# A hybrid decoder step on one core: dt behind the short convolution, state transposes between state updates, placeholder rows in quarters

## The chip, the cores and the metric

The kernel runs on one core of a Trainium2 chip. A core has a matrix engine (TensorE, PE in the profile), VectorE (DVE), ScalarE (ACT), GpSimd (POOL) and a queue engine that issues most of the transfers (SyncE, SP); each follows its own instruction list and waits on semaphores. The metric is the device time of one execution in microseconds (us).

## The reference, cut to what matters

One layer for 528 prompt tokens (16 learned ones ahead of 512) and 64 sample tokens (8 sequences of 8), 592 in all, width 1024, all in float32:

```python
h = RMSNorm(x)
z, xbc, dt_raw, sc_b, sc_c, sc_h, g_ssd, g_sc = split(h @ w_in)   # dt_raw: 32 columns
xbc = silu(causal_conv4(xbc) + conv_b)
dt = softplus(dt_raw + dt_bias);  a_neg = -exp(A_log)
acum = cumsum(dt * a_neg)                # in chunks of 128 tokens
y, state = chunked_scan(x, dt, acum, B, C, state0) ; y += x * D
y_ssd = group_rmsnorm(y * silu(z)) @ w_ssd_out
y_sc = (sc_b * causal_conv3(sc_c * sc_h)) @ w_sc_out
x = x + (sigmoid(g_ssd) * y_ssd + sigmoid(g_sc) * y_sc) @ w_o
x = x + moe(RMSNorm(x))                  # 4 groups of 8 experts, top 1 group, top 2 experts
```

Final states and the last rows before each convolution are outputs too.

## The kernel before, in words

Each engine's program is written out by hand. The work is in stages.

**Start.** SyncE loads the first tile of rows, then eleven small vectors and the dt weights `wdt`, then the other four tiles, then the first weight blocks. Five tiles of 128 rows (the last has 80: 16 of the prompt and 64 of the samples) are normed: ScalarE sums the squares of a row and takes the root (`root`, L1425 and L1426), VectorE scales the rows (L1013), TensorE transposes them (L602), VectorE multiplies by the norm's weights into `hT` (L1004). A float32 product is then made of three faster ones: weights and activations are split into a rounded part (`w_hi`, `hT_hi`, by ScalarE, L1438 and L1444) and the rest (`w_lo`, `hT_lo`, a subtraction on GpSimd, L1691 and L1697). In the start all five row sums come first, then the first two weight roundings, then the five of h; GpSimd does the two weight subtractions and then the five of h. The dt product alone is made in plain float32, token tile by token tile (L610), then the small vectors are transposed (L617, L621), and VectorE and ScalarE make dt and dt*a of it.

**Blocks.** `pe_block` (L578) multiplies one block of 128 weight columns with all 592 tokens: 8 row tiles x 3 products x 2 halves of the tokens, 48 matmuls. Raw weights have two places in `ring`, and so do the split ones. When TensorE has finished block n, ScalarE rounds block n+2, GpSimd subtracts, and SyncE loads block n+4 into the place that came free. 24 blocks are the short convolution's (a loop of 4 turns of 6), 16 are the gate and `w_sc_out` (8 turns of 2), and the cumulative sums of dt stand between the two (L636 to L640).

**Groups.** Four turns of a loop follow, one per head group: ten blocks (C, B, four x, four z) with the convolution on VectorE (L1118, L1120), the chunked scan over the five tiles, and a tail. Before this loop ScalarE's queue issues six copies of input rows into `y_tok` (L1494), a table in device memory that only the experts' gather at the end reads, as placeholders that must be finite. In the scan, ScalarE copies B (L1532) and takes the exp of each half of the heads (L1536), for which TensorE's next decay matmul (L672) waits. In the last tile TensorE updates the eight sample states in four pieces (L745): pieces 2 and 3 wait until VectorE has added pieces 0 and 1 (L1173, L1174), since they use the same banks. Then come the transposes of the output tokens (L753) and of the prompt's state (L759, into bank `pT`), then one block for the next group (L578), then the row sums for the group norm (L770). SyncE stores the sample states after the fourth addition (L470) and only then loads the next weights.

After the groups come 24 more blocks, `w_o`, the router, and 16 pairs of experts.

## Time and profile before

| | |
|---|---|
| three runs | 1444.98, 1453.1, 1454.42 us (median 1453.1) |
| profiled execution | 1448.88 us, its span 1447.1 us |
| TensorE busy | 1339.0 us, 93% of the span |
| VectorE, ScalarE, GpSimd busy | 563.5, 379.3, 458.9 us |
| granted TensorE clock, mean | 0.945 |

A busy TensorE isn't TensorE at its peak: the matmuls are pipelined and their ends are modelled. The granted clock is given as a share of 2.4 GHz; 0.50 is the lower level of 1.2 GHz. A stage's bound is read from what TensorE waits for in that stage.

### The profile page before, as it was taken

What the parts mean: (1) busy time and instruction counts of PE and PEld (TensorE: products, weight loads), DVE (VectorE), ACT (ScalarE), POOL (GpSimd) and SP (SyncE); (2) the same over time, 40 slices, a digit from 0 to 9 for tenths busy, and PEclk for the clock granted to TensorE, in tenths of its full rate; (3) what the DMA queues carried; (4) which work ended last, traced back from release to release, by engine and by line L of the source; (5) the groups of instructions that cost most, each with busy time, mean ns of one, the idle gap of its engine ahead of it and who ended that gap; (6) DMA issues with size and microseconds to landing.
All of it is one profiled execution on the core that took longest, in us unless ns stands there. A gap on an engine that the chain in (4) does not pass through costs nothing.

```text
span 1447.1 us, 23251 instructions
## 1 busy us (share of the span) xinstructions
PE 1339.0 (93%) x9114; PEld 1039.5 (72%) x9114; DVE 563.5 (39%) x814; ACT 379.3 (26%) x573; POOL 458.9 (32%) x379
## 2 busy tenths in 40 slices
PE   6999999998989898999989899999987999999990
PEld 5999999998759876976887699995474444444430
DVE  3454440015555754864585560011153111111115
ACT  4212123443333423533242351210121111111102
POOL 5244433334341532543163254340001222222110
PEclk8899999999998999999899999999966999999995
DMA  5123223247106303510541222336711999999925
GB/s 142 45 73 87 72 73 87 73 138 201 45 1 167 87 14 91 133 43 0 144 109 43 65 73 73 88 117 206 318 53 37 378 366 356 373 362 371 380 103 204
DMA packets 179364, 209.54 MB, mean 145 GB/s; under 512 B 13019, under 2 KB 154459, under 8 KB 170959
## 3 DMA queue, kind: packets, MB, share of 16 engines
q1 hardware_dynamic: 168010, 188.05, 39.4%
q10 hardware_dynamic: 4126, 10.83, 2.2%
q0 software_dynamic: 7168, 9.81, 1.9%
q8 instruction: 43, 0.70, 0.2%
q14 instruction: 17, 0.14, 0.0%
HBM read 196.73 MB, written 32.15 MB: 158 GB/s over the span
## 4 chain that ended last, share of the span: by engine, by line
PE 74%; DVE 12%; issue 5%; DMA 4%; ACT 3%; SPq 1%; DVEq 1%; POOL 0%; ACTq 0%; POOLq 0%
PE acc L578 34%; PE pT L921 8%; PE acc L796 5%; DVE area L1120 4%; PE pS L934 4%; PE acc L960 4%; DMA ring<-in_w_in 3%; PE pY L728 2%; PE pS L968 2%; PE pS L672 2%; PE acc L897 1%; PE acc L694 1%; PE pO L610 1%; DVE big L1191 1%; PE pY L904 1%
## 5 line engine op out<-in xcount | busy, mean ns | idle before, releaser
L578 PE MATMUL acc<-h_parts,ring_parts 128*128 128x328 f32 (+1 forms) x3840 | 550.6, 305 | 9.4 <-POOL ring_parts L1691 8.6
L578 PEld LDWEIGHTS acc<-h_parts,ring_parts 128*128 128x128 f32 x3840 | 536.9, 192 | 22.4 <-issue 21.6
L1691 POOL TENSOR_TENSOR ring_parts<-ring,ring_parts 128x1024 fp32r<-128x1024 f32 x104 | 262.8, 2527 | 427.4 <-ACT ring_parts L1438 427.3
L1438 ACT ACTIVATE ring_parts<-ring 128x1024 fp32r<-128x1024 f32 x104 | 110.0, 1058 | 359.9 <-PE acc L578 326.9
L921 PE MATMUL pT<-area,big 128*64 128x512 f32 x384 | 116.2, 612 | 0.3 <-ACT big L1620 0.3
L578 PE MATMUL acc<-u_parts,ring_parts 128*128 128x264 f32 (+1 forms) x640 | 109.5, 299 | 0.0
L1120 DVE SCALAR_TENSOR_TENSOR area<-area,xvec 128x616 f32<-128x616 f32 x72 | 94.2, 1309 | 10.5 <-DVE area L1118 0.6
L578 PEld LDWEIGHTS acc<-u_parts,ring_parts 128*128 128x128 f32 x640 | 96.4, 188 | 0.0
L921 PEld LDWEIGHTS pT<-area,big 128*64 128x64 f32 x384 | 35.2, 140 | 79.2 <-issue 79.2
L578 PE MATMUL acc<-area_parts,ring_parts 128*128 128x264 f32 (+1 forms) x512 | 91.2, 299 | 0.0
L578 PEld LDWEIGHTS acc<-area_parts,ring_parts 128*128 128x128 f32 x512 | 78.4, 188 | 0.0
L1837 POOL DMA_INDIRECT big<-h_rows,gid_main x16 | 16.7, 1042 | 161.7 <-DVE big L1322 107.5
L934 PE MATMUL pS<-area,big 128*32 128x256 f32 x768 | 58.5, 381 | 0.0
L960 PE MATMUL acc<-area,big 128*64 128x512 f32 x192 | 58.4, 599 | 0.0
L921 PE MATMUL pT<-ring,big 128*64 128x512 f32 x128 | 56.7, 596 | 0.0
L1764 POOL TENSOR_TENSOR area<-m_le,da 128x512 f32<-128x512 f32 (+1 forms) x40 | 41.1, 1031 | 47.6 <-PE pS L672 47.6
L1632 ACT ACTIVATE big<-pT 128x256 f32<-128x256 f32 x16 | 6.1, 383 | 190.6 <-PE pT L921 190.6
L1858 POOL DMA_INDIRECT y_tok<-big,sid_over x16 | 16.0, 998 | 124.4 <-DMA y_tok<-big,sid_main 124.4
L672 PE MATMUL pS<-area,m_gt 128*128 128x512 f32 (+1 forms) x80 | 39.1, 570 | 12.7 <-ACT area L1536 12.7
L1211 DVE TENSOR_TENSOR area<-acc,area 128x528 f32<-128x528 f32 x8 | 5.7, 708 | 115.7 <-PE acc L578 115.7
L1353 DVE TENSOR_TENSOR big<-big,pT 128x256 f32<-128x256 f32 x16 | 6.7, 421 | 111.5 <-ACT big L1632 111.5
L1151 DVE TENSOR_TENSOR area<-area 128x512 f32<-128x512 f32 (+1 forms) x40 | 36.4, 919 | 32.2 <-ACT area L1536 30.7
(320 smaller groups left out, 1727.2 us busy)
## 6 DMA issues: line engine op xcount, KB each, us to landing
ring<-in_w_in SPq DMA_DIRECT2D x80, 512.0 KB, 4.0
area<-in_w_gate SPq DMA_DIRECT2D x24, 1024.0 KB, 6.6
area<-in_w_up SPq DMA_DIRECT2D x24, 1024.0 KB, 9.3
area<-in_w_down SPq DMA_DIRECT2D x24, 1024.0 KB, 10.6
area<-in_state_ssm SPq DMA_DIRECT2D x16, 512.0 KB, 7.1
out<-area SPq DMA_DIRECT2D x16, 512.0 KB, 6.4
ring<-in_w_ssd_out SPq DMA_DIRECT2D x16, 512.0 KB, 3.6
ring<-in_w_gate SPq DMA_DIRECT2D x8, 1024.0 KB, 11.2
```

The lines of the kernel that those rows point to most:

```text
L578: m = nc.tensor.matmul(acc[a][:, h, 0:n], w[s][:, k, :], x[:, k, h * HALF:h * HALF + n], start=first and k == 0 and w is w_hi and x is hi, ...
L672: nc.tensor.matmul(pS[0:r, 0:4 * r], gt[0:r, 0:r], rbuf[0:r, q, 0:4 * r], start=True, stop=True).then_inc(p_seg, 1)
L728: m = nc.tensor.matmul(pY[0:r, h * HD:(h + 1) * HD], wts[0:r, h // 4, (h % 4) * r:(h % 4 + 1) * r], xdt[0:r, i % 2, h * HD:(h + 1) * HD], ...
L796: m = nc.tensor.matmul(acc[n % 4 // 2][0:ROWS[i], n % 2, :], mT[:, k, tok(i)], wo[h][:, k, :], start=k == 0, stop=k == 7)
L921: m = nc.tensor.matmul(pT[main_of(j), :], xT_[:, k, main_of(j)], gate_up_w(2 * p + j, k), start=k == 0, stop=k == 7)
L934: m = nc.tensor.matmul(pS[over_of(q), 0:FE], xT_[:, k, at:at + OVER], wexp[(2 * p + j) % 4][n][:, k, :], start=k == 0, stop=k == 7)
L960: m = nc.tensor.matmul(acc[1][main_of(j), h, :], hT_main[:, ft, main_of(j)], wexp[(2 * p + j) % 4][2][:, ft, h * 512:(h + 1) * 512], start ...
L1120: x = v.scalar_tensor_tensor(o_, raw[:, c % 2, n:n + XCONV], w[:, 0, n:n + 1], o_, ALU.mult, ALU.add)
L1151: v.tensor_tensor(w, w, cbm[0:r, 0:r].unsqueeze(1).broadcast_to([r, 4, r]), ALU.mult).then_inc(s_w, 1)
L1438: a_.activation(w_hi[b % 2], w_raw[b % 2], ACT.Copy).then_inc(hi_done, 1)
L1691: gp.tensor_tensor(w_lo[b % 2], w_raw[b % 2], w_hi[b % 2].bitcast(F32), ALU.subtract).then_inc(lo_done, 1)
L1764: gp.tensor_tensor(rbuf[0:r, q, 0:4 * r].rearrange("p (h c) -> p h c", h=4), le[0:r, 0:r].unsqueeze(1).broadcast_to([r, 4, r]), da[0:r, i, ...
```

## The change

It has four parts. The inputs are loaded in another order: all token rows, then the first two weight blocks, then the vectors; three small vectors come over ScalarE's queue, which also loads its square-root table before the rows are there. On ScalarE all row sums stand before the weight roundings, with the first two roundings of h between them; GpSimd subtracts for h tiles 0 and 1, then for weight blocks 0 and 1, and VectorE subtracts for h tiles 2 to 4. The dt product is made in split form like a block, heads by tokens, after the 24 blocks of the short convolution; its result is copied out and transposed back, and the softplus and the cumulative sums stand after the first and the second turn of the gate loop, which are unrolled. In the tail of a group the transposes stand between the state updates, into bank `pS`, and the next block waits for the third state addition alone. The placeholder rows are written in four parts, one in each group's turn, after its first z block, from one stretch of the prompt's rows.

```diff
@@ sync
+            for i in range(1, 4):
+                r0 = i * P - N_META
+                sp.dma_start(x_tok[:, i, :], xp[r0:r0 + P, :]).then_inc(x_in[i], 16)
...
+            for n in range(2):
+                load_block(s_block(0, n), n, w_in_cols(s_cols[n], P))
             sp.dma_start(v3[0:4, :], ins["ssd_conv_w"][0]).then_inc(vec_in, 16)
...
             sp.dma_start(wdt, w_in_cols(COL_DT, HEADS)).then_inc(vec_in, 16)
...
@@ tensor
-            for i in range(TILES):
-                for k in range(8):
-                    m = nc.tensor.matmul(pO[0:ROWS[i], i * HEADS:(i + 1) * HEADS], hT[:, k, tok(i)], wdt[:, k, :],
-                                         start=k == 0, stop=k == 7)
...
             pe.wait_ge(h_lo, TILES)
             with pe.Fori(0, 4) as t:
                 for b in range(6):
                     pe_block(pe, s_block(t, b), b, hT_hi, hT_lo)
 
+            pe.wait_ge(s_wdt, 2)
+            for k in range(8):
+                at = slice(k * HEADS, k * HEADS + P)
+                for n, (w, x) in enumerate(((wdt_hi, hT_hi), (wdt_hi, hT_lo), (wdt_lo, hT_hi))):
+                    nc.tensor.matmul(pT[:, 0:HALF], w[:, at], x[:, k, 0:HALF], start=k + n == 0, stop=k == 7 and n == 2)
+                    m = nc.tensor.matmul(pS[:, 0:T - HALF], w[:, at], x[:, k, HALF:T], start=k + n == 0, stop=k == 7 and n == 2)
+            m.then_inc(s_dtmm, 1)
...
+            vectors(0, pY)
...
+            o1_turn(0)
+            pe.wait_ge(s_dtrow, 1)
+            vectors(12, pS)
+            pe.wait_ge(s_vcp, 2)
+            for i in range(TILES):
+                m = nc.tensor.transpose(pO[0:ROWS[i], i * HEADS:(i + 1) * HEADS], dt_rows[0:HEADS, tok(i)],
+                                        ident[0:HEADS, 0:HEADS])
+            m.then_inc(s_dtmm, 1)
+            o1_turn(1)
             pe.wait_ge(s_dtv, 3)
...
-                        for k in range(GK):
-                            if k >= 2:
-                                pe.wait_ge(s_hs, g * 4 + (k - 1))
...
+                        state_update(0)
+                        state_update(1)
+
                     pe.wait_ge(s_y2, g * 5 + (i + 2))
...
                 pe.wait_ge(s_st, g * 6 + 6)
+                for k in range(GK):
+                    m = nc.tensor.transpose(pS[:, k * P:(k + 1) * P], st[:, k * P:(k + 1) * P], ident[:, :])
+                m.then_inc(p_so, 1)
+                for k in range(2, GK):
+                    pe.wait_ge(s_hs, g * 4 + (k - 1))
+                    state_update(k)
+
                 pe.wait_ge(s_hs, g * 4 + 3)
...
+                pe_block(pe, g_block(g, 10), 10, hT_hi, hT_lo)
                 pe.wait_ge(s_hs, g * 4 + 4)
...
@@ vector
+            for i in range(2, TILES):
+                dve.wait_ge(h_hi, i + 1)
+                v.tensor_tensor(hT_lo[:, :, tok(i)], hT[:, :, tok(i)], hT_hi[:, :, tok(i)].bitcast(F32), ALU.subtract
+                                ).then_inc(h_lo, 1)
@@ scalar
+            a_.preload_act_table(ACT.Sqrt)
...
             for i in range(TILES):
                 act.wait_ge(x_in[i], 32 if i in (0, 4) else 16)
                 root(i, x_tok[0:ROWS[i], i, :], junk, s_sd)
+                if i in (2, 3):
+                    h_split(i - 2)
...
-            for n in range(2):
-                at = n * Y_ROWS
-                for rows, x in ((slice(0, N_META), ins["meta_tokens"]), (slice(N_META, TP), ins["x_prompt"][0]),
-                                (slice(TP, T), ins["x_sample"].rearrange("b s d -> (b s) d"))):
-                    act.dma_start(y_tok[at + rows.start:at + rows.stop, :], x).then_inc(y_fill, 16)
...
                 z_gate(0)
+                act.dma_start(y_tok[bass.ds(g * (DUMP // GROUPS), DUMP // GROUPS), :], ins["x_prompt"][0][0:DUMP // GROUPS, :]
+                              ).then_inc(y_fill, 16)
@@ gpsimd
-            for b in range(2):
-                split_lo(s_block(0, b), b, 0)
-            for i in range(TILES):
+            for i in range(2):
                 pool.wait_ge(h_hi, i + 1)
...
+            for b in range(2):
+                split_lo(s_block(0, b), b, 0)
```

TensorE's own order at the start, in the kernel before, up to the loop over the short convolution's blocks (`acc` rows are the transposes of h, `pO` rows the dt product, `pT`, `pY` and `pS` rows the vectors):

```order
L602 MATMUL acc<-ident,area 128x128 x32
L602 MATMUL acc<-ident,area 128x80 x8
L610 MATMUL pO<-area,big 128x32 x32
L610 MATMUL pO<-area,big 80x32 x8
L617 MATMUL pT<-ident,area 128x2 x16
L621 MATMUL pY<-ident,area 128x29 x12
L621 MATMUL pS<-ident,area 128x29 x12
L625 UNCONDITIONAL_BRANCH
```

and in the changed kernel:

```order
L608 MATMUL acc<-ident,area 128x128 x32
L608 MATMUL acc<-ident,area 128x80 x8
L612 UNCONDITIONAL_BRANCH
L612 ISA
L578 ISA
```

The dt product and the vectors are gone from between the transposes of h and the loop. They stand after it.

TensorE in the tail of a group before (L745 are the state updates, three matmuls to a piece, L753 the token transposes, L759 the state transposes, L578 the next block):

```order
L745 MATMUL pO<-area 128x256
L743 ISA
L745 MATMUL acc<-area 128x512
L745 MATMUL acc<-area 128x256
L745 MATMUL pT<-area 128x256
L743 REGISTER_ALU
L745 MATMUL acc<-area 128x512
L745 MATMUL acc<-area 128x256
L745 MATMUL pO<-area 128x256
L753 MATMUL pY<-ident,area 128x80 x4
L759 MATMUL pT<-ident,area 128x128 x4
L578 MATMUL acc<-h_parts,ring_parts 128x264
```

and in the changed kernel (L764, L773, L778 and L584 in this order):

```order
L764 MATMUL pO<-area 128x256
L773 MATMUL pY<-ident,area 128x80 x4
L776 REGISTER_ALU
L778 MATMUL pS<-ident,area 128x128 x4
L781 ISA
L764 MATMUL acc<-area 128x512
L764 MATMUL acc<-area 128x256
L764 MATMUL pT<-area 128x256
L764 MATMUL acc<-area 128x512
L764 MATMUL acc<-area 128x256
L764 MATMUL pO<-area 128x256
L584 MATMUL acc<-h_parts,ring_parts 128x264
```

Both sets of transposes stand between the second and the third update, and the block follows the fourth.

ScalarE in the scan of a group, changed kernel (L1554 and L1555 copy the first z block, L1577 copies B, L1581 is the exp):

```order
L1554 ACTIVATE area<-acc 128x528
L1555 ACTIVATE area<-acc 128x64
L1572 ISA
L1572 DMA y_tok<-in_x_prompt 32x9856
L1576 REGISTER_ALU
L1577 ACTIVATE area<-pO 128x128
L1580 REGISTER_ALU
L1581 ACT_TABLE_LOAD
L1581 ACTIVATE area<-pS 128x512
```

The transfer of the placeholder rows is issued between the z copy and the copy of B; before, nothing stood there.

## Rows read from the trace of the kernel before

**Rows 1.** The page's chain that ended last: share of the span by engine.

```profile
PE 74%; DVE 12%; issue 5%; DMA 4%; ACT 3%; SPq 1%; DVEq 1%; POOL 0%; ACTq 0%; POOLq 0%
```

**Rows 2.** Timeline, TensorE, 23 to 60 us: start, duration, line, tiles, count, idle before.

```profile
23.39 15.99 PE L610 MATMUL pO<-area,big 128*128 128x32 f32 x80 [1.09 <-DVE big L1004]
39.32 1.86 PE L617 MATMUL pT<-ident,area 2*128 2x2 f32 x16
41.05 1.46 PE L621 MATMUL pY<-ident,area 29*128 29x29 f32 x12
...
43.71 16.54 PE L578 MATMUL acc<-h_parts,ring_parts 128*128 128x264 f32 x110
```

**Rows 3.** Timeline, ScalarE, 5 to 24 us.

```profile
5.97 1.28 ACT L1425 ACT_TABLE_LOAD   x1 [5.97 <-DMA area<-in_x_prompt]
...
8.44 1.28 ACT L1426 ACT_TABLE_LOAD   x1
...
12.31 0.29 ACT L1426 ACTIVATE stat<-stat,eps 128x1 f32<-128x1 f32 x1
...
13.68 0.29 ACT L1426 ACTIVATE stat<-stat,eps 128x1 f32<-128x1 f32 x1
...
20.07 4.51 ACT L1444 ACTIVATE h_parts<-big 128x1024 fp32r<-128x1024 f32 x5
```

**Rows 4.** GpSimd's timeline, and VectorE's row scaling by its line (ns: least/median/most).

```profile
18.57 5.13 POOL L1691 TENSOR_TENSOR ring_parts<-ring,ring_parts 128x1024 fp32r<-128x1024 f32 x2 [13.90 <-ACT ring_parts L1438]
23.66 11.76 POOL L1697 TENSOR_TENSOR h_parts<-big,h_parts 128x1024 fp32r<-128x1024 f32 x5
L1013 DVE TENSOR_SCALAR area<-area,stat x5: 752/754/2443, 10.3 to 19.0; 128x1024 f32<-128x1024 f32 x4, 80x1024 f32<-80x1024 f32 x1
```

**Rows 5.** Timeline, VectorE, a two-input operation while GpSimd is idle.

```profile
868.79 0.77 DVE L1214 TENSOR_TENSOR big<-big,area 128x592 f32<-128x592 f32 x1
```

**Rows 6.** Stretches: busy time of each engine, then PEclk, DMA share, GB/s.

```profile
24.00:26.00 2.00, 2.00 (x12) 2.00 (x11) 0.79 (x1) 1.86 (x2) 2.00 (x1) 0.50 0.53 124
```

**Rows 7.** The chain of waits: the short convolution's 24 blocks.

```profile
43.78 158.58 PE acc L578 x1152
```

**Rows 8.** Weight loads of 296 to 345 us, issue to landing; TensorE's timeline there.

```profile
DMA to landing us min/median/max: 3.9/4.2/16.3
...
340.98 25.45 PE L578 MATMUL acc<-h_parts,ring_parts 128*128 128x264 f32 x168 [4.12 <-POOL ring_parts L1691]
```

**Rows 9.** Group 0: the six issues by line; timelines of TensorE, SyncE and ScalarE.

```profile
L1494 ACTq DMA_DIRECT2D y_tok<-in_x_prompt x2: 597/608/619, 317.9 to 319.8; - x2
...
370.21 1.10 PE L672 MATMUL pS<-area,m_gt 128*128 128x512 f32 x2 [1.79 <-ACT area L1536]
370.07 0.37 SPq L433 DMA_DIRECT2D ring<-in_w_in  x1
375.83 1.06 ACT L1438 ACTIVATE ring_parts<-ring 128x1024 fp32r<-128x1024 f32 x1 [3.89 <-PE acc L578]
379.84 0.28 ACT L1532 ACTIVATE area<-pO 128x128 f32<-128x128 f32 x1 [2.34 <-PE pO L663]
```

**Rows 10.** Timeline, TensorE, first transposes of group 1's scan.

```profile
495.97 0.66 PE L659 MATMUL pT<-ident,area 128*128 128x128 f32 x4 [0.89 <-ACT area L1503]
```

**Rows 11.** Timelines, tail of group 1: TensorE's third update and next block, VectorE's fourth addition.

```profile
561.04 0.69 PE L745 MATMUL acc<-area 32*128 32x512 f32 x2 [2.19 <-DVE area L1174]
...
565.90 8.08 PE L578 MATMUL acc<-h_parts,ring_parts 128*128 128x264 f32 x48
...
564.38 0.95 DVE L1173 TENSOR_TENSOR area<-area,acc 128x768 f32<-128x768 f32 x1 [0.79 <-PE pO L745]
```

**Rows 12.** After group 0's tail: a stretch, the chain's ring load, TensorE's timeline.

```profile
442.00:444.00 2.00, 2.00 (x15) 2.00 (x15) 0.00 (x0) 1.87 (x1) 0.00 (x0) 0.88 0.95 285
444.61 6.65 DMA ring<-in_w_in
472.29 22.80 PE L578 MATMUL acc<-h_parts,ring_parts 128*128 128x264 f32 x168 [1.51 <-POOL ring_parts L1691]
```

201 lines of the change are left out of this document (111 added, 90 removed).

## The prediction

> **What bounds the kernel now.** I read the page's chain of waits first: 74% of the span is on TensorE and 5% is issue, so a step counts only if TensorE's own queue waits for it or executes it [rows 1]. Then the timeline, stage by stage, for the places where TensorE is idle or does slow work. There are four.
>
> At the start, TensorE multiplies the dt columns in plain fp32 from 23.39, 80 matmuls in 15.99 us, then transposes the vectors, and the first dense weight block begins at 43.71 [rows 2]. The granted clock is at its lower level of 1.2 GHz in this stretch (0.50 in 24 to 26 us) [rows 6]. ScalarE paces the row sums ahead of it, and it pays a table load of 1.28 us before the first square and another before the first root [rows 3].
>
> At the first group, one weight load lands 16.3 us after its issue where the median is 4.2; TensorE waits 4.12 us, and then takes 25.45 us for 168 matmuls [rows 8]. The six copies of the placeholder rows were issued just before.
>
> In the scan of each group the second decay matmul waits for ScalarE, 1.79 us in group 0 [rows 9]. At the tail of each group TensorE waits 2.19 us for VectorE between the second and third state update, then for the third and fourth, and only then transposes and starts the next block [rows 11].
>
> **The sum, part by part**, against the profiled execution's own 1448.9 us. It lies 4.2 below the median shown (1453.1); the mean of the three runs is 1450.8, and I carry the difference onto that mean, since two of the three lie high and one low.
>
> *Start: the first block.* The input rows are issued ahead of the vectors, and both table loads leave ScalarE's path (one load of the square-root table is issued before the rows arrive). Rows arrive at 5.97 as before [rows 3]. ScalarE then has five row sums at a pace of 1.37 (12.31 to 13.68 [rows 3]), five roundings of h, 4.51 together [rows 3], and two weight roundings of 1.06: 6.9 + 4.5 + 2.1 = 13.5, so 19.5. The last tile's trip through VectorE, the transposes and VectorE again adds about 2.3: 21.8. GpSimd's part can begin once the first tile is rounded, at about 12.7: two h subtractions of 2.35 (11.76 for five) and two weight subtractions of 2.57 (5.13 for two) [rows 4] are 9.9. VectorE takes the other three h subtractions, by 0.77 for 592 columns [rows 5] about 1.3, 1.3 and 0.8, or 3.4. Do the two engines shut each other out? The row scaling on VectorE takes 0.75 and, at the time of GpSimd's first subtraction, 2.44 [rows 4]. So one end is 21.8 and most of the 3.4, or 24.5, and the other is all of it in series with three row scalings of 0.75: 12.7 + 9.9 + 3.4 + 2.3 = 28.3. I take 26.5, in the middle, a little to the late side: 43.7 - 26.5 = 17.2 off.
>
> The clock: before, TensorE had little to do around 20 us and was at 0.50 from 24 [rows 6]. The first blocks will find the same, with less dense work ahead of them than the blocks at 43.71 had. After the 4.12 us wait, 168 matmuls took 25.45 [rows 8] where 3.5 blocks of 6.6 [rows 7] are 23.1: a loss of 2.3. The old first blocks bore a part of such a loss; I take 1.5 more, ends 0 and 2.3.
>
> *Start: what comes back.* The dt product becomes 48 matmuls in the form of a block. Twenty-four blocks take 158.58 [rows 7], so 6.6. The vector transposes, 1.86 and twice 1.46 at the low clock [rows 2], move between dense blocks; at full clock they lie between 2.4 and 4.8, and five dt transposes add some 0.6. I take 3.0, ends 3.0 and 5.4. The softplus chain, three table loads of 1.28 [rows 3] and some fourteen small operations of a few tenths each, needs an estimated 8 us after the first gate turn and is covered by the second turn's two blocks (13.1); without that cover it would stop TensorE at the cumulative sums, where the wait for it now stands. The sums themselves move by a turn and cost the same. The broadcast of D goes to GpSimd and the splitting of the dt weights to ScalarE and GpSimd, behind the first two blocks' splits and before the third's, which nobody wants until the first block is done: nothing, with 6.6 us of cover. Start in all: -17.2 + 1.5 + 6.6 + 3.0 = **-6.1**.
>
> *The placeholder rows.* Without six copies in front of it the load lands in some 4 us, and the 4.12 wait and the 2.3 behind it go: -6.4. What is late next is the chain of convolutions, since in group 1 TensorE waits 0.89 for it before the scan [rows 10]; I leave that much in: **-5.5**. The copies come back as one issue a group on ScalarE's queue, 0.61 each [rows 9], between the first z copy and the copy of B. That place is on the path: ScalarE goes without a pause into the table load and the exp for which TensorE waits. So 4 x 0.61 = **+2.4**; nothing if ScalarE's issue is hidden, which no row suggests. The transfer itself: a quarter of the 12.1 us by which the one load was late is 3.0. The load beside it is issued at 370.07 and by the 4.2 is there at 374.3; ScalarE wants it at 375.83, and after that has 2.34 of idle before the next B copy [rows 9]. That is 3.8 of cover for 3.0: nothing. The same bytes go over the same queues by the Trainium skill, page DMA: Bandwidth & Descriptors, section Issuing engines are not separate DMA queues, which says that transfers from any engine share the 16 DMA engines and interleave. By that page alone the quarters save nothing that they do not hide, which is a rival below.
>
> *The group tails.* The token transposes and the four state transposes now fill the 2.19 us wait and the one behind it, and the next block needs only the third state addition, not the fourth: it starts at the end of the third, 1.6 us earlier in group 1 (565.90 against 564.3, where the fourth update ends) [rows 11]. In groups 0 to 2 that isn't yet a gain. The chain behind it goes through the fourth addition: four stores, the ring load (6.65), ScalarE's rounding and square root, VectorE's convolutions, and TensorE waits 1.51 for them later [rows 12]. An earlier block lengthens that wait. The chain itself gets shorter by the state output of 256 KB, which now goes ahead of the stores: 0.9 at the 285 GB/s of that stretch [rows 12], an estimate. If the filled wait also keeps the clock up, the fourth addition no longer waits 0.79 for TensorE [rows 11]: 1.7. In group 3 nothing is loaded behind it, and the whole counts: 1.6, or 3.1 if the block runs in 6.6 and not 8.08 [rows 11]. So 3 x 0.9 + 1.6 = 4.3 at the low end, 3 x 1.7 + 3.1 = 8.2 at the high one; no row says whether the clock holds, so the middle: **-6.3**.
>
> Sum: -6.1 - 5.5 + 2.4 - 6.3 = -15.5. On the profiled execution 1433.4; on the mean of the runs **1435.3**. Its own range, by the ends above, is 1428 to 1441.
>
> **Rivals.** *Everything at its good end*: first block at 24.5 and no clock loss (-9.6), the whole 6.4, tails 8.2, against the 2.4 of issue: -21.8, or 1429.0. For it: no row shows VectorE's subtraction of this shape blocked. Chance 0.12.
>
> *The start is spent on the shared work of VectorE and GpSimd.* The 2.44 against 0.75 [rows 4] is a delay of 1.7; if two more such fall on the chain and all is in series, the first block is at 32, 5.5 later than taken: 1440.8. Against it: before, the start was on TensorE and not there. Chance 0.18.
>
> *The quarters don't hide.* All of the 12.1 us falls on TensorE over the four turns, by a load each that is in use sooner than I think: 1435.3 + 12.1 = 1447.4. This is what the skill's DMA page would make of it if there were no cover; the rows show 3.8 of it. Chance 0.10.
>
> *Slower: each quarter holds up a load as the whole did.* Place: the first z weights in each scan. Price: 12.1 of delay less 3.8 of cover is 8.3, four times 33.2, so 1468.5. It decides from the point where that load lands over 8.0 us after its issue. For it: the copy now goes out as few very long pieces, beside a load of small ones, and nothing says that the delay is in proportion to bytes. Against it: the late load landed together with the end of the stall, so the six copies were then gone, and each quarter is a quarter of their bytes. Chance 0.04.
>
> That the change doesn't do what it says, the row sums still waiting for the input rows, is within the second rival's time.
>
> **How the numbers follow.** A run of this kernel can tell about 1% from no change, here 14.5 us, so the line is 1438.6. Forecast 0.56, of which four fifths lie below the line (0.45); good end 0.12; a fifth of the second rival (0.04): faster 0.61. Slower 0.04. The rest is within 1%: 0.35. The range leaves out the slower case, the upper part of the unhidden one and the tip of the good end: 1424 to 1446.
>
> **What would show it.** In the changed profile: the first dense block between 24.5 and 28.3; a dt product of about 6.6 us after the twenty-fourth block and no idle time at the cumulative sums; no wait over 1 us for a weight load in group 0's convolutions; a ScalarE DMA issue of 0.6 in each scan and the second decay matmul's wait longer by it; the wait in the tails below 0.5, and the clock after it; TensorE's wait for GpSimd in the next group's third or fourth block grown to 2 or more. I am wrong if the first block is past 30, if a load in a scan lands after 8 us, or if the tails' gain comes in full in groups 0 to 2 too.

## The result, and the profile after

The changed kernel takes **1428.62 us** (median of 4 runs, 1426.42 to 1430.33) against 1450.72 for the kernel before on the same chip (4 runs, 1444.98 to 1454.42). The ratio is 0.986, 95% interval 0.9836 to 0.9884: 1.4% faster. The profiled execution took 1430.2, with a span of 1428.5 against 1447.1. The medians lie 22.1 us apart, the ratio stands for 20.3, and the two traces, which show where the time went, for 18.6.

The chain that ended last hardly changes its shape [rows 1]:

```profile
PE 75%; DVE 12%; issue 4%; ACT 3%; DMA 3%; SPq 1%; DVEq 1%; ACTq 0%; POOLq 0%; POOL 0%
```

**Start.** Three timelines of the changed kernel: TensorE, VectorE and GpSimd (start, duration, line, operation, tiles, count, idle before). They answer [rows 2] and [rows 4].

```profile
27.02 33.23 PE L584 MATMUL acc<-h_parts,ring_parts 128*128 128x264 f32 x227 [6.88 <-DVE h_parts L1047]
```
```profile
14.55 1.42 DVE L1036 TENSOR_SCALAR area<-area,stat 128x1024 f32<-128x1024 f32 x1
17.20 1.55 DVE L1036 TENSOR_SCALAR area<-area,stat 80x1024 f32<-80x1024 f32 x1
20.91 5.75 DVE L1047 TENSOR_TENSOR h_parts<-big,h_parts 128x1024 fp32r<-128x1024 f32 x3
```
```profile
18.16 6.17 POOL L1736 TENSOR_TENSOR ring_parts<-ring,ring_parts 128x1024 fp32r<-128x1024 f32 x2
24.29 1.70 POOL L1748 TENSOR_TENSOR area_parts<-area,area_parts 128x256 fp32r<-128x256 f32 x1
```

The first dense block begins at 27.02 instead of 43.71, and VectorE's three h subtractions, 5.75 us, are the last thing it waits for. GpSimd's two weight subtractions, of which the second runs beside them, take 6.17 where they took 5.13 [rows 4].

TensorE further on: the dt product ran from 186.26 to 192.87, and behind it stand the small transposes.

```profile
192.87 1.15 PE L625 MATMUL pO<-ident,area 2*128 2x2 f32 x16
193.88 0.91 PE L631 MATMUL pY<-ident,area 29*128 29x29 f32 x12
...
208.00 0.92 PE L631 MATMUL pS<-ident,area 29*128 29x29 f32 x12
208.76 0.45 PE L646 MATMUL pO<-ident,area 32*128 32x32 f32 x5
```

Stretches of the same kernel (busy time of each engine, then PEclk, the granted TensorE clock, then DMA share and GB/s): ahead of the first block, in it, and in the block behind the cumulative sums. The last two lines are new: behind its sums the kernel before had a clock of 1.00, and the block there took 6.6 us where it now takes 8.2.

```profile
24.00:26.00 2.00, 0.00 (x0) 0.00 (x0) 2.00 (x2) 0.00 (x0) 2.00 (x3) 0.50 0.35 70
30.00:32.00 2.00, 2.00 (x12) 2.00 (x11) 0.00 (x0) 0.00 (x0) 0.00 (x0) 0.62 0.00 0
226.00:228.00 2.00, 2.00 (x10) 2.00 (x10) 0.33 (x1) 0.77 (x4) 0.02 (x1) 0.52 0.16 49
228.00:230.00 2.00, 2.00 (x12) 2.00 (x12) 0.00 (x0) 0.00 (x0) 0.00 (x0) 0.63 0.71 213
```

**Group 0.** TensorE runs into the scan without a wait for a weight load. Its next rows, and ScalarE's with ScalarE's own queue (ACTq), answer [rows 8] and [rows 9]:

```profile
354.99 0.65 PE L678 MATMUL pT<-ident,area 128*128 128x128 f32 x4
...
358.64 1.10 PE L691 MATMUL pS<-area,m_gt 128*128 128x512 f32 x2 [1.80 <-ACT area L1581]
```
```profile
353.89 0.73 ACT L1545 ACTIVATE area<-area,xvec 128x528 f32<-128x528 f32 x1 [5.90 <-DVE area L1149]
354.34 0.67 ACTq L1572 DMA_DIRECT2D y_tok<-in_x_prompt  x1
354.53 0.33 ACT L1546 ACTIVATE area<-area,xvec 128x64 f32<-128x64 f32 x1
354.77 1.04 ACT L1468 ACTIVATE ring_parts<-ring 128x1024 fp32r<-128x1024 f32 x1
```

The DMA issue, 0.67 us, stands on ScalarE's queue at 354.34. ScalarE's datapath, the part that computes, is then in the first of two silus and still has the rounding and the two z copies to do, to 356.41. All of them stand ahead of the issue in the program, so the queue runs ahead of the datapath. TensorE's wait for the exp is 1.80, against 1.79 before.

**Tails.** TensorE in group 1's tail, against [rows 11]; then its wait in group 2's blocks, against [rows 12].

```profile
547.15 0.66 PE L778 MATMUL pS<-ident,area 128*128 128x128 f32 x4
548.35 0.69 PE L764 MATMUL acc<-area 32*128 32x512 f32 x2 [0.54 <-DVE area L1203]
...
551.06 7.97 PE L584 MATMUL acc<-h_parts,ring_parts 128*128 128x264 f32 x48 [0.20 <-DVE area L1203]
...
584.68 7.62 PE L584 MATMUL acc<-h_parts,ring_parts 128*128 128x264 f32 x54 [2.02 <-POOL ring_parts L1736]
```

The 2.19 wait is 0.54, yet the block behind it still takes 7.97 where a block at full clock takes 6.6. The clock does hold for longer than it did. Four state transposes of the kernel before, then a stretch of each kernel around its transposes, before and after (the clock is the third number from the end):

```profile
564.83 1.06 PE L759 MATMUL pT<-ident,area 128*128 128x128 f32 x4
```
```profile
563.00:565.00 2.00, 2.00 (x11) 0.76 (x6) 1.21 (x3) 0.00 (x0) 0.00 (x0) 0.50 0.00 0
```
```profile
547.00:549.00 2.00, 1.36 (x11) 0.72 (x10) 2.00 (x4) 0.60 (x1) 0.38 (x1) 1.00 0.00 0
```

The same transposes take 0.66 at a clock of 1.00, where they took 1.06 at 0.50. In groups 0 and 2 the block is slower than it was: 9.2 against 8.5, and 9.2 against 8.3.

**Where 18.6 us came from.** I compare starts of the same work on TensorE, before minus after; call the difference the lead. It is 16.7 at the first block. At the start of group 0's blocks it is 310.51 - 305.98 = 4.5. At group 0's scan it is 366.57 - 354.99 = 11.6, so 7.1 came from the placeholder rows. At the updates at the scan's end it is 429.11 - 417.55 = 11.6, so nothing was lost in the scan. The four tails add 1.1, 1.9, 1.6 and 2.2, which are 6.8 in all, and the lead is 18.4 behind the last of them.

### The profile page after: what moved, and what is told of

It reads as the page before. It is cut to its first block, busy times and chain, and to the rows that moved or that the text cites. A ratio compares the mean times of both kernels' runs of the same rounds, so it can differ in the third digit from the quotient of the medians.

```text
span 1428.5 us, 23149 instructions
## 1 busy us (share of the span) xinstructions
PE 1324.7 (93%) x9087; PEld 1027.3 (72%) x9087; DVE 567.5 (40%) x816; ACT 377.9 (26%) x574; POOL 457.0 (32%) x380
## 4 chain that ended last, share of the span: by engine, by line
PE 75%; DVE 12%; issue 4%; ACT 3%; DMA 3%; SPq 1%; DVEq 1%; ACTq 0%; POOLq 0%; POOL 0%
PE acc L584 36%; PE pT L944 8%; PE acc L819 5%; PE pS L957 4%; PE acc L983 4%; DVE area L1149 4%; PE pY L747 2%; PE pS L991 2%; PE pS L691 2%; DMA ring<-in_w_in 1%; PE acc L920 1%; PE acc L713 1%; DVE big L1220 1%; PE pY L927 1%; PE pS L753 1%
## 5 line engine op out<-in xcount | busy, mean ns | idle before, releaser
L584 PE MATMUL acc<-h_parts,ring_parts 128*128 128x328 f32 (+1 forms) x3840 | 551.5, 305 | 12.6 <-DVE h_parts L1047 6.9
L584 PEld LDWEIGHTS acc<-h_parts,ring_parts 128*128 128x128 f32 x3840 | 537.7, 192 | 29.0 <-issue 28.2
L584 PE MATMUL acc<-u_parts,ring_parts 128*128 128x264 f32 (+1 forms) x640 | 109.4, 299 | 0.0
L584 PEld LDWEIGHTS acc<-u_parts,ring_parts 128*128 128x128 f32 x640 | 96.4, 188 | 0.0
L1149 DVE SCALAR_TENSOR_TENSOR area<-area,xvec 128x616 f32<-128x616 f32 x72 | 90.1, 1252 | 10.5 <-DVE area L1147 0.6
L584 PE MATMUL acc<-area_parts,ring_parts 128*128 128x264 f32 (+1 forms) x512 | 91.1, 299 | 0.0
L584 PEld LDWEIGHTS acc<-area_parts,ring_parts 128*128 128x128 f32 x512 | 78.4, 188 | 0.0
L1890 POOL DMA_INDIRECT big<-h_rows,gid_main x16 | 16.7, 1043 | 161.9 <-DVE big L1351 107.6
L1911 POOL DMA_INDIRECT y_tok<-big,sid_over x16 | 16.0, 998 | 125.1 <-DMA y_tok<-big,sid_main 125.1
```

Source lines behind the costliest of these rows:

```text
L584: m = nc.tensor.matmul(acc[a][:, h, 0:n], w[s][:, k, :], x[:, k, h * HALF:h * HALF + n], start=first and k == 0 and w is w_hi and x is hi, ...
L1149: x = v.scalar_tensor_tensor(o_, raw[:, c % 2, n:n + XCONV], w[:, 0, n:n + 1], o_, ALU.mult, ALU.add)
```

## The experiments

Each is an edit of the changed kernel. Three series shared their chips with the kernel before (medians 1447.9, 1447.7, 1449.2, and 1448.0 for the last run). The changed kernel itself was not in them; by its ratio it would be at 1427.4 to 1428.9 there. With the intervals of both ratios, a difference from it is uncertain by some 4 us. Where less is claimed below, it rests on the traces.

**The three parts one by one.** The placeholder rows back:

```diff
             split_hi(g_block(0, 0), 0)
+            for n in range(2):
+                at = n * Y_ROWS
+                for rows, x in ((slice(0, N_META), ins["meta_tokens"]), (slice(N_META, TP), ins["x_prompt"][0]),
+                                (slice(TP, T), ins["x_sample"].rearrange("b s d -> (b s) d"))):
+                    act.dma_start(y_tok[at + rows.start:at + rows.stop, :], x).then_inc(y_fill, 16)
             with act.Fori(0, GROUPS) as g:
...
                 z_gate(0)
-                act.dma_start(y_tok[bass.ds(g * (DUMP // GROUPS), DUMP // GROUPS), :], ins["x_prompt"][0][0:DUMP // GROUPS, :]
-                              ).then_inc(y_fill, 16)
```

> The changed kernel with the placeholder rows as before: six copies in front of group 0, none in the scans. My theory, from the lead that TensorE gained in group 0: that part is worth 7.05 us, so this kernel takes about 1428.6 + 7 = 1435.6, a weight load in group 0 lands about 16 us after its issue again and TensorE waits about 4 us for it. Rival A, the price in the prediction: 5.5 less 2.4 for four issues, so 3.1, or 1431.7. Rival B, the whole is hidden now because TensorE arrives at another moment: 1428.6 and no such wait.

1435.48 (5 runs), ratio 0.9909 [0.9893, 0.9925]. Two rows of it: its two weight loads issued from 315 to 330 us, issue to landing, and TensorE.

```profile
DMA to landing us min/median/max: 11.7/14.2/16.7
```
```profile
337.17 24.98 PE L584 MATMUL acc<-h_parts,ring_parts 128*128 128x264 f32 x168 [4.52 <-POOL ring_parts L1739]
```

The wait is back and so are 7.1 us by the ratios (0.9909 / 0.986). The ratios alone, uncertain by 4 us, hardly exclude the prediction's net 3.1; the trace does. From the start of group 0's blocks to its scan this kernel takes 56.0 (306.30 to 362.29), the kernel before 56.1 and the changed kernel 49.0. My theory holds.

The tails back:

```diff
-                        state_update(0)
-                        state_update(1)
+                        for k in range(GK):
+                            if k >= 2:
+                                pe.wait_ge(s_hs, g * 4 + (k - 1))
+                            state_update(k)
...
                 pe.wait_ge(s_st, g * 6 + 6)
-                for k in range(GK):
-                    m = nc.tensor.transpose(pS[:, k * P:(k + 1) * P], st[:, k * P:(k + 1) * P], ident[:, :])
-                m.then_inc(p_so, 1)
-                for k in range(2, GK):
-                    pe.wait_ge(s_hs, g * 4 + (k - 1))
-                    state_update(k)
-                pe.wait_ge(s_hs, g * 4 + 3)
+                pe.wait_ge(s_hs, g * 4 + 3)
+                for k in range(GK):
+                    m = nc.tensor.transpose(pT[:, k * P:(k + 1) * P], st[:, k * P:(k + 1) * P], ident[:, :])
+                m.then_inc(p_so, 1)
+                pe.wait_ge(s_hs, g * 4 + 4)
                 pe_block(pe, g_block(g, 10), 10, hT_hi, hT_lo)
```

> The changed kernel with the group tails as before: all four state updates together, then the state transposes, then the next block. My theory, from the leads gained group by group: 6.8 us over the four groups (1.1, 1.9, 1.6, 2.2), so 1435.4, with the 2.2 us wait between the second and third update back. Rival: the part was worth only the low end of the prediction, 4.3, since the chain through the fourth addition to the next group's convolutions is what ends last: 1432.9.

1436.03 (5 runs), ratio 0.9917 [0.9902, 0.9933], 8.3 slower by the ratios and 5.9 by the spans (1434.4 against 1428.5); 6.8 lies between. TensorE's waits, 370 to 440 us:

```profile
PE acc L765 <- DVE area L1200: 2.2, 1, 2.2
```

From the updates to the next scan, the first three tails together take 198.8, against 199.5 in the kernel before and 194.9 in the changed one.

The start alone (both edits above together):

> The start of the changed kernel alone; placeholder rows and tails as before. My theory: the first dense block at 27, 16.7 us earlier, of which 4.5 are left at group 0, so 1450.7 - 4.5 = 1446.2, and the three parts add up to the whole. The block behind the cumulative sums is where 1.6 us of the predicted 6.1 go, in a stretch of low granted clock; that stretch should be here too, since it has nothing to do with the other two parts. Rival: the parts cover for each other, so that the start alone brings all 6.1 (1444.6), or nothing (1450.7).

1442.4 (8 runs), ratio 0.9965 [0.9953, 0.9977]: 5.1 us, with an interval of 3.3 to 6.8 that excludes neither 4.5 nor 6.1. 5.1, 7.1 and 8.3 make 20.5, against 20.3 for the whole. Within their intervals the parts add up, and nothing shows that they cover for each other. The stretch at the lower clock behind the sums is there, as expected: the block takes 8.1 (225.98 to 234.12). But in the kernel with the tails back, whose start is the same, it is missing: there the block takes 6.6 (226.70 to 233.33), after 24 first blocks that took 159.8 instead of 159.2. So where that stretch falls differs between executions of one and the same start. The start was taken whole: what the order of the loads, the early table load and the new place of the dt product bring each isn't shown.

**The issue on ScalarE.** The same bytes in four DMAs instead of one:

```diff
-                act.dma_start(y_tok[bass.ds(g * (DUMP // GROUPS), DUMP // GROUPS), :], ins["x_prompt"][0][0:DUMP // GROUPS, :]
-                              ).then_inc(y_fill, 16)
+                for p4 in range(4):
+                    act.dma_start(y_tok[bass.ds(g * (DUMP // GROUPS) + p4 * (DUMP // GROUPS // 4), DUMP // GROUPS // 4), :],
+                                  ins["x_prompt"][0][p4 * 77:p4 * 77 + 77, :]).then_inc(y_fill, 16)
```

> The changed kernel with each group's share of the placeholder rows in four DMAs of 77 rows instead of one of 308, at the same place in ScalarE's program; the same bytes. My theory: ScalarE's queue issues a DMA while earlier activations still run, 0.3 us of cover for one issue and no more. One issue then costs 0.3 at most and four of 0.6 cost the rest: 4 groups x up to 3 x 0.6 = 7.2, less the wait for the cumulative sum on TensorE that ScalarE has ahead of the B copy (2.3 us of idle before the second B copy in the kernel before): I expect 0 to 4, say 1430.5. Rival, the prediction's reading that every issue is on the path: 12 more issues x 0.6 = 7.2, so 1435.8. Rival, an issue never costs anything there: 1428.6 and the waits for the decay exp unchanged at 1.8.

1438.24 (6 runs), ratio 0.9935 [0.9918, 0.9952]: 10.9 us slower by the ratios and 8.2 by the spans, more than any of the three theories said. ScalarE in group 0, both its datapath and its queue:

```profile
354.82 0.67 ACTq L1573 DMA_DIRECT2D y_tok<-in_x_prompt  x1
355.00 0.33 ACT L1546 ACTIVATE area<-area,xvec 128x64 f32<-128x64 f32 x1
355.24 1.04 ACT L1468 ACTIVATE ring_parts<-ring 128x1024 fp32r<-128x1024 f32 x1
355.66 0.53 ACTq L1573 DMA_DIRECT2D y_tok<-in_x_prompt  x1
356.19 0.59 ACT L1554 ACTIVATE area<-acc 128x528 f32<-128x528 f32 x1
356.36 0.52 ACTq L1573 DMA_DIRECT2D y_tok<-in_x_prompt  x1
356.68 0.21 ACT L1555 ACTIVATE area<-acc 128x64 f32<-128x64 f32 x1
357.37 0.54 ACTq L1573 DMA_DIRECT2D y_tok<-in_x_prompt  x1
358.02 0.28 ACT L1578 ACTIVATE area<-pO 128x128 f32<-128x128 f32 x1 [1.13 <-issue]
```

One issue is covered whole; of four, 1.13 us sticks out. TensorE's wait for the exp grows from 1.80 to 3.04 in group 0 and to 2.7 in the others, which is 4.0 us in four groups. The rest of what the scans lose is the clock. TensorE and then the granted clock in group 1, of this kernel, and the same stretch in the changed kernel:

```profile
487.76 1.10 PE L691 MATMUL pS<-area,m_gt 128*128 128x512 f32 x2 [2.72 <-ACT area L1582]
```
```profile
489.00:492.00 3.00, 3.00 (x10) 2.26 (x9) 2.38 (x3) 0.50 (x1) 1.04 (x1) 0.50 0.41 119
492.00:495.00 3.00, 3.00 (x21) 3.00 (x21) 0.00 (x0) 0.04 (x1) 0.00 (x0) 0.93 0.00 0
```
```profile
489.00:492.00 3.00, 3.00 (x22) 3.00 (x21) 2.09 (x3) 0.00 (x0) 0.34 (x1) 1.00 0.42 126
```

0.9 us more of waiting (2.72 against 1.80) is followed by 1.7 us of lost clock. From scan start to updates the changed kernel's groups take 62.6, 60.9, 62.6 and 60.9 us, at a mean clock of 0.97, 1.00, 0.97 and 1.00. Here they take 62.1, 65.1, 66.6 and 63.4, at 1.00, 0.95, 0.92 and 0.97: 10.4 more in all. Group 0 shows that the clock need not fall: its wait grew most, and its scan was not longer. The next kernel, with the same four issues, repeats all four times within 0.1.

**Bytes and place.** As the last, but 308 rows in each of the four DMAs, so 5.05 MB a group (the table `y_tok` is made larger for them):

```diff
-                    act.dma_start(y_tok[bass.ds(g * (DUMP // GROUPS) + p4 * (DUMP // GROUPS // 4), DUMP // GROUPS // 4), :],
-                                  ins["x_prompt"][0][p4 * 77:p4 * 77 + 77, :]).then_inc(y_fill, 16)
+                    act.dma_start(y_tok[bass.ds(g * DUMP + p4 * (DUMP // GROUPS), DUMP // GROUPS), :],
+                                  ins["x_prompt"][0][0:DUMP // GROUPS, :]).then_inc(y_fill, 16)
```

> As the kernel with four DMAs a group, but each of the four copies 308 rows instead of 77: four times the bytes in each scan, 5.05 MB, about what the six copies of the kernel before moved at once. Theory 1, delay in proportion to bytes with a fixed cover: the load beside it is late by some 12.1 us, ScalarE can spare 3.8, so each group loses 8.3 and the kernel takes 1438.2 (four DMAs, 77 rows) + 33 = 1471; the z weights then land at 16 us or later. Theory 2, at this place nobody needs a load for so long that even the whole is hidden: 1438.2. I hold the first. If a group loses more than 8.3, the lower granted clock behind the added idle time adds to it.

1438.5 (5 runs), ratio 0.993 [0.9907, 0.9952]: four times the bytes cost nothing that shows beside the last kernel's 0.9935, and my theory, which said 33 us, falls. The weight load issued at 359.08, to landing, and ScalarE's rounding that uses it:

```profile
DMA to landing us min/median/max: 16.7/16.7/16.7
```
```profile
379.31 1.06 ACT L1468 ACTIVATE ring_parts<-ring 128x1024 fp32r<-128x1024 f32 x1 [3.97 <-PE acc L584]
```

The load is about as late as the one before the change [rows 8], and ScalarE still waits for TensorE, not for it: landed at 375.8, wanted at 379.3.

The other way round, the quarter at the old place:

```diff
             with act.Fori(0, GROUPS) as g:
+                act.dma_start(y_tok[bass.ds(g * (DUMP // GROUPS), DUMP // GROUPS), :], ins["x_prompt"][0][0:DUMP // GROUPS, :]
+                              ).then_inc(y_fill, 16)
...
                 z_gate(0)
-                act.dma_start(y_tok[bass.ds(g * (DUMP // GROUPS), DUMP // GROUPS), :], ins["x_prompt"][0][0:DUMP // GROUPS, :]
-                              ).then_inc(y_fill, 16)
```

> The changed kernel with each group's quarter of the placeholder rows issued at the start of the group, ahead of its x blocks, where the kernel before had the whole of them for all groups, instead of in the scan. Theory: size is enough on its own. The whole made one load 12.1 us late and cost a wait of 4.1, so 8 us of lateness are covered there; a quarter makes 3.0 and costs nothing in group 0, 1427.6 to 1428.6 as the changed kernel. Rival: place is what matters, and there each load that comes later than the 4 us of its row is waited for: in group 0 up to 3.0, and in the later groups, where TensorE waits 1.3 to 2.0 for a chain that begins with a ring load, up to 3 more each, so up to 1440.

1427.59 (5 runs), ratio 0.9851 [0.9828, 0.9874], the changed kernel's time. No weight load of 300 to 350 us takes longer than 6.8 us here, nor in the changed kernel, and from the start of group 0's blocks to its scan both take 49.0. So the smaller size is enough by itself. The place is enough by itself too, by the kernel with four times the bytes, apart from the price of its four issues. The change does both.

**VectorE beside GpSimd at the start.**

```diff
-            for b in range(2):
-                split_lo(s_block(0, b), b, 0)
+            split_lo(s_block(0, 0), 0, 0)
+            pool.wait_ge(h_lo, TILES)
+            split_lo(s_block(0, 1), 1, 0)
```

> The changed kernel, but GpSimd's subtraction for the second weight block waits until VectorE has done its three h subtractions. It isn't wanted before the first block is done, 13 us later at the low clock. Theory (the second rival of the prediction, in part): VectorE and GpSimd hold each other up; VectorE's three subtractions take 5.75 us beside GpSimd's work where 3.4 was the price by a row without company. Alone they take at most 1.3 each and the first block begins 1.5 to 2.3 us earlier, at about 25. Rival: the subtraction into the rounded type costs 1.9 by itself: first block at 27.0 as now, nothing gained. What is gained at the first block should be kept to group 0, as half of it was lost to nothing but clock.

1425.88 (4 runs), ratio 0.9858 [0.9827, 0.9889]. The median decides nothing; the trace does. VectorE, GpSimd and TensorE:

```profile
21.43 3.08 DVE L1047 TENSOR_TENSOR h_parts<-big,h_parts 128x1024 fp32r<-128x1024 f32 x3
```
```profile
18.66 2.83 POOL L1736 TENSOR_TENSOR ring_parts<-ring,ring_parts 128x1024 fp32r<-128x1024 f32 x1
24.59 2.36 POOL L1736 TENSOR_TENSOR ring_parts<-ring,ring_parts 128x1024 fp32r<-128x1024 f32 x1 [3.10 <-DVE h_parts L1047]
```
```profile
24.85 11.41 PE L584 MATMUL acc<-h_parts,ring_parts 128*128 128x264 f32 x71 [4.21 <-DVE h_parts L1047]
```

The same three subtractions take 3.08 alone and 5.75 beside GpSimd, as the theory said. Most of the difference is in one of them: in the changed kernel the second ran from 22.05 to 25.41, 3.36 us instead of 1.22, while GpSimd's second weight subtraction ran from 20.95 to 24.33. The block begins 2.2 earlier, and group 0's scan 2.7 earlier (352.27). The rest of this execution's 5.2 us lies in later stages, which the edit doesn't touch.

**The sums a turn later.**

```diff
             o1_turn(1)
+            o1_turn(2)
             pe.wait_ge(s_dtv, 3)
...
-            with pe.Fori(2, 8) as f:
+            with pe.Fori(3, 8) as f:
```

The same is done on VectorE and ScalarE.

> The changed kernel with the cumulative sums, and what ScalarE and VectorE do for them, one gate turn later: behind the third turn instead of the second. Theory: the 1.6 us that the block behind the sums loses at a granted clock of 0.5 comes from the stretch of small transposes and sums before it, so that a turn (13 us) of dense blocks more between the transposes and the sums keeps the clock up and group 0 starts 1.6 earlier, at 353.4. Rival: the sums themselves bring the clock down wherever they stand: 355.0 as in the changed kernel, and the same block loses 1.6 a turn later.

1430.21 (4 runs), ratio 0.9885 [0.9861, 0.991]. The stretch behind the sums, in their new place:

```profile
242.00:244.00 2.00, 2.00 (x17) 2.00 (x16) 0.00 (x0) 0.00 (x0) 0.00 (x0) 1.00 0.83 239
```

The clock stays up there. From the last sum to the scan it takes 114.7 and, with the turn of 13.1 that now stands ahead of the sums, 127.8, against 129.3: 1.5 us is saved. But the first block began 0.8 later in this execution and the 24 blocks took 0.6 more, so group 0's scan began at 354.89 and not at the 353.4 expected. The scan itself took 64.2 instead of 62.6, with a longer stretch at the lower clock around 408 us. So the drop is not the sums' own, and the kernel without it ends no earlier: both spans are 1428.5. Why the lower clock came back 165 us later stays open.

**The chain behind the tails.**

```diff
+            def load_x(g, k):
+                load_block(g_block(g, 2 + k), k, w_in_cols(g * GW + (COL_X + k * P), P))
...
-                for k in range(GK):
-                    load_block(g_block(g, 2 + k), k, w_in_cols(g * GW + (COL_X + k * P), P))
+                for k in range(2, GK):
+                    load_x(g, k)
...
                     load_cb(g + 1)
+                    for k in range(2):
+                        load_x(g + 1, k)
                 hold(sp, s_hs, g * 4 + 4)
...
             load_cb(0)
+            for k in range(2):
+                load_x(0, k)
```

> The changed kernel with the first two x weight loads of the next group issued ahead of the four state stores instead of behind them. Theory, the reason given for the tails of groups 0 to 2: what ends last there is the chain fourth state addition, four stores, ring load, ScalarE's rounding and square root, VectorE's normalization and convolutions. The ring load lands at 438.6 in the changed kernel, where TensorE's sums of squares end at 438.65; without the wait ScalarE rounds from 434.5 and the square root comes 1.1 to 2.3 us earlier, so TensorE's waits of 1.3 to 2.0 for GpSimd in the next group's blocks and part of the 0.9 before the scan go: 3 x 1.1 to 3 x 2.9, so 1428.6 - 3.3 to - 8.7. Rival: the chain through VectorE (reciprocal 3.85, scaling 5.2, convolutions) is bound by the square root's own inputs and the waits stay: 1428.6. Against a gain too: the stores come later, and the next load of states may wait for them.

1422.07 (4 runs), ratio 0.9824 [0.98, 0.9848], 5.2 better than the changed kernel by the ratios, with an uncertainty of nearly as much, and 7.7 by the spans. ScalarE and TensorE behind group 0's tail:

```profile
432.69 1.06 ACT L1475 ACTIVATE ring_parts<-ring 128x1024 fp32r<-128x1024 f32 x1 [1.60 <-PE acc L591]
...
436.59 0.48 ACT L1615 ACTIVATE area<-pT,eps 128x264 f32<-128x264 f32 x1 [1.54 <-PE pS L800]
```
```profile
436.14 26.05 PE L591 MATMUL acc<-h_parts,ring_parts 128*128 128x264 f32 x188
```

In the changed kernel the rounding waited 5.83 us for the ring load, to 438.58, and the square root began at 440.95, 2.3 after its sums were there. Here both wait for TensorE alone, and TensorE's waits for GpSimd and for the convolutions are gone in every group: from scan to scan 123.4, 125.9 and 123.4 instead of 128.3, 125.1 and 127.5. The middle one shows no gain, although its 2.02 us wait is gone too. Each of these three stretches holds a scan, which takes 60.9 or 62.6 by its clock, and here the middle one had the slower scan. Without the scans they are 62.5, 63.3 and 62.5 instead of 65.8, 64.2 and 64.9, so all three are shorter.

**A faster version.** Both edits together:

> The changed kernel with both edits that gained: GpSimd's second weight subtraction waits for VectorE's h subtractions, and the next group's first two x loads go ahead of the state stores. The two are 400 us apart. Theory: they add up, 1425.9 and 1422.1 against 1427.6 to 1428.6 for the changed kernel, so 1422.1 - 2.2 = 1419.9, with the first block at 25 and no wait for GpSimd in the groups' blocks. Rival: the earlier first block only moves the lower-clock stretches about, and the gain over 1422.1 is between 0 and 1.

1421.04 (5 runs), ratio 0.9798 [0.9774, 0.9822]. The first block is at 24.73, but the span, 1420.8, is that of the last kernel, as the rival said. It is 2.9 ahead of that kernel at group 0's scan and 0.1 at group 3's.

Then ScalarE's z copy, its rounding and the DMA behind the first exp:

```diff
                 silu(5)
-                z_gate(0)
-                act.dma_start(y_tok[bass.ds(g * (DUMP // GROUPS), DUMP // GROUPS), :], ins["x_prompt"][0][0:DUMP // GROUPS, :]
-                              ).then_inc(y_fill, 16)
...
                         a_.activation(wts[0:r, q, 0:4 * r], pS[0:r, 0:4 * r], ACT.Exp).then_inc(s_exp, 1)
+                        if i == 0 and q == 0:
+                            z_gate(0)
+                            act.dma_start(y_tok[bass.ds(g * (DUMP // GROUPS), DUMP // GROUPS), :],
+                                          ins["x_prompt"][0][0:DUMP // GROUPS, :]).then_inc(y_fill, 16)
```

> The kernel with both edits, and in each scan ScalarE's copy of the first z block, with its rounding and the DMA of the placeholder rows, moved behind the first decay exp instead of ahead of the copy of B. Theory: TensorE's 1.8 us wait for the exp in each group is ScalarE's queue of work ahead of it: 1.04 rounding, 0.6 and 0.2 copies, then 0.3 and a table load of 1.28. Without the first three, 1.8 us, the exp ends about 1.3 to 1.8 earlier: 4 x 1.3 to 4 x 1.8, so 5.2 to 7.2 off, about 1414. Rival: the same work then stands between the first exp and the second, and TensorE waits there instead: 1.84 of work against the 1.1 to 1.3 that ScalarE idles there, 0.6 lost a group, and GpSimd's subtraction for the third z block comes 3 us later; the gain is then 2 to 4, or nothing if the z block's part is wanted sooner.

1417.81 (5 runs), ratio 0.9779 [0.9756, 0.9801]. The median gains 3.2, less than forecast, and the intervals of the two ratios overlap. Of the 1.84 us of work taken out of the way ScalarE now idles 1.15 for the transpose of B, with the table load still to come, and TensorE's wait only falls from 1.80 to 1.51, so 1.2 in four groups. The span gains 6.6 (1414.2 against 1420.8), but most of that is clock, a mean of 0.956 against 0.951, and whether the edit brings it isn't shown. Last, the table load put into that hole:

```diff
                 silu(5)
+                a_.preload_act_table(ACT.Exp)
```

> The last kernel (z copy behind the first exp) with one line more: the exp table's load is issued right behind the last silu of each group's convolutions, in the 1.15 us in which ScalarE waits for the transpose of B, instead of between the copy of B and the first exp. Theory: what was left of TensorE's wait for that exp, 1.51 us a group, is the table load of 1.28; of it 1.15 is now covered. 4 x 1.15 = 4.6 less, so about 1417.8 - 4.6 = 1413.2, and the wait at 0.4. Rival: the copy that follows brings its own table with it, the load is made twice, and nothing is gained or 1.3 a group lost (1423). A smaller rival: with less idle time fewer stretches at the lower clock, 1.6 less for each.

1414.04 (6 runs), ratio 0.9772 [0.9749, 0.9794]. ScalarE, then TensorE:

```profile
353.19 1.28 ACT L1578 ACT_TABLE_LOAD   x1
354.49 0.28 ACT L1582 ACTIVATE area<-pO 128x128 f32<-128x128 f32 x1
355.19 0.60 ACT L1586 ACTIVATE area<-pS 128x512 f32<-128x512 f32 x1 [0.42 <-PE pS L698]
```
```profile
355.93 1.10 PE L698 MATMUL pS<-area,m_gt 128*128 128x512 f32 x2 [0.78 <-ACT area L1586]
```

The wait went 1.80, 1.51, 0.78. It was expected at 0.4; now the exp itself waits 0.42 for TensorE's matmul. The rival, that the table is loaded twice, is out. (The Trainium skill, page ScalarE: Activation LUTs, section Table sets: the hidden batching unit, says that copy is in every set; the copy at 354.49 agrees, since no load stands between it and the exp.) The forecast gain of 4.6 isn't shown: by their ratios the last two can't be told apart, and their spans are 1414.2 and 1412.5. The last three scans took 59.9 each, the first 63.1, with more of the lower clock. Either is faster than both kernels that are compared here: the last is 2.3% faster than the kernel before.

## Why the prediction was right, and where not

1433.4 was forecast for the profiled execution and 1430.2 came; 1435.3 for the runs and 1428.6 came. By its steps:

**Start, -6.1 forecast, 4.5 found.** The first block was taken at 26.5 and began at 27.0. The 24 blocks lost 0.7 more to the clock than before (159.2 against 158.5), where 1.5 was forecast. The dt product took 6.6 and the small transposes 3.0 (1.85 and 1.14 between the starts of what stands around them), both as forecast. When the sums and two gate turns were done the lead was 231.95 - 225.81 = 6.1, the forecast, in part because two small misses cancelled. What failed is that the sums "move by a turn and cost the same". They themselves took 3.5 us in both kernels, but the block behind them took 1.6 more, at the lower clock. The sums' experiment, and the kernel with the tails back, show that this isn't the sums' doing; that it can be saved to the end, neither shows. The exclusion of VectorE and GpSimd was real, 2.7 us in the three subtractions. Without it the block began at 24.85, close to the end of 24.5 that the prediction gave for no exclusion; that the middle between its two ends came out is a guess that went well. The price for the three alone was 3.4, against 3.08 measured. The Trainium skill (page GPSIMD Engine Reference, section Key points) says that GpSimd contends with VectorE's instructions with two SBUF inputs, which these have; the trace agrees, with 3.08 against 5.75.

**Placeholder rows, -5.5 forecast, 7.1 found.** The wait and the lower clock behind it went, as forecast. The clock's part was mis-sized: without the wait of 4.1 the kernel before would take 51.9 from the start of the blocks to the scan, against 49.0 now, so it was some 2.9 and not 2.3. The 0.9 that I held back for the convolutions wasn't waited for in group 0 and belongs to the later groups alone.

**ScalarE's issue, +2.4 forecast, 0 found.** This step is wrong. It read "ScalarE goes without a pause into the table load", and took a queue's issue for time of the engine. The row of the changed kernel shows the issue under a silu; the four-DMA kernel shows that the cover ends, since of four issues' 2.3 us 1.1 stuck out.

**Cover for the quarter.** Its result, nothing, was right, its 3.8 us of cover wrong. I paired the load issued at 370.07 with the rounding at 375.83 [rows 9], but the ring holds two blocks: that load serves the rounding after it, at 389.0, so the cover was 14.7. The slower rival rested on the same number: a landing over 8.0 would decide. In the four-times kernel it landed at 16.7, and nothing was lost. The Trainium skill (page DMA: Bandwidth & Descriptors, section Issuing engines are not separate DMA queues) says that DMAs started by different engines run on the same 16 DMA engines and interleave. The trace agrees: the copies on ScalarE's queue make SyncE's load 12.6 us late. What fails is the cover that the prediction set against it, since two loads' lead hides the whole.

**Tails, -6.3 forecast, 6.8 found.** Right in sum, for partly wrong reasons. The prediction has TensorE wait again "for the third and fourth" addition; the kernel before shows no such wait, and its block at 565.90 follows without idle time [rows 11]. Whether the clock holds was left open and the middle taken. It holds through the transposes of group 1 (1.00 for 0.50) and not in the block, which still takes 8.0 in groups 1 and 3. Groups 0 to 2 gained 1.1, 1.9 and 1.6, where 0.9 was the low end and 1.7 the high one, and group 3 gained 2.2. A gain in full in groups 0 to 2 was named as a sign of being wrong; with full at 1.6 it came in two of the three. The mechanism behind the middle, a chain of stores, ring load, rounding and square root, is shown by the kernel that takes the load out of it. The sign that I named, GpSimd's wait grown to 2 or more, came in one group of three (1.31, 2.02, 1.28).

So the 3.2 us by which the profiled execution beat its forecast are 2.4 of an issue that costs nothing, 1.6 too little for the rows and 0.5 for the tails, less 1.6 lost at the start; the 0.3 left is rounding and what came behind the tails. On the medians the miss is 6.7. The other 3.5 is where the two profiled executions happened to lie, this one 1.6 above its median and the one before 1.9 below the mean that I carried the sum onto.

Two things about the number are luck or loose. The median, 1428.6, is within half a microsecond of the rival in which everything comes at its good end (1429.0), but that rival's conditions didn't come: the first block was at 27.0 and not 24.5, the clock loss was not nothing, and the tails were 6.8 and not 8.2. And the line of 1438.6 between faster and the same was reckoned from the median of 1453.1, while the forecast was reckoned from the mean of 1450.8. From that mean the line is 1436.3, barely above the forecast of 1435.3, so the share of four fifths below the line was too high.

## What to carry to other kernels

Before a transfer in front of others is priced, find out which later instruction reads the late load, counting the buffers between, since here the same 12 us of lateness cost a stall at one place and nothing at another. On ScalarE's queue one DMA issue was free while ScalarE had work queued in front of it, and of four in a row half was not; look at what the engine still has to do before you price an issue. An added wait of TensorE can cost more than itself: four waits that grew by 4.0 us in all came with 10.4 us of longer scans, the rest by a lower clock, though in one group of the four the clock did not fall. And since a scan of the same work takes 60.9 or 62.6 in one and the same kernel, compare stage by stage before a few microseconds of span are credited to an edit.

## What was not expected of the hardware

- ScalarE's queue issued a DMA (0.67 us) while two silus, a rounding and two copies that precede it in the program were still to finish. Of four issues' 2.3 us, 1.13 showed as idle time of the datapath.
- Scans of the same work and with the same waits take 60.9 or 62.6 us, and one took 64.2 (group 1 of the kernel with the placeholder rows back). The steps of about 1.6 us go with the granted clock, which was 1.00, 0.97 and 0.95.
- VectorE's subtraction of 128x1024 with a rounded result: three take 3.08 us alone, 5.75 beside a GpSimd subtraction; GpSimd's own goes from 2.36 to 3.38.
- The exp's table load can be made ahead of a plain copy and stays in place through it: 1.28 us at 353.19, and none before the exp.
